# Layer 1's sixteen experts: gate and up products by seven products of quarters, the down product from turned gated rows

## What is computed

```python
def expert_choice_ffn(h, w_router, w_gate, w_up, w_down):
    b, n, _ = h.shape
    cap = CAPACITY_FACTOR * n // N_EXPERTS
    aff = jax.nn.softmax(jnp.einsum('bnd,de->bne', h, w_router).astype(jnp.float32), axis=-1)
    gate, idx = lax.top_k(jnp.swapaxes(aff, 1, 2), cap)
    bidx = jnp.arange(b)[:, None, None]
    xg = h[bidx, idx]
    hid = jax.nn.silu(jnp.einsum('becd,edf->becf', xg, w_gate)) * jnp.einsum('becd,edf->becf', xg, w_up)
    out = jnp.einsum('becf,efd->becd', hid, w_down) * gate[..., None].astype(h.dtype)
    return jnp.zeros_like(h).at[bidx, idx].add(out)
```

## Time and profile before

| | us |
|---|---|
| median of three runs | 3442.67 (3441.97 to 3445.3) |
| the profiled execution, its own time | 3441.68 |
| its span, first to last instruction | 3440.0 |
| TensorE busy (matmul) | 3204.8, 93% |
| VectorE busy | 1227.8, 36% |
| ScalarE busy | 934.1, 27% |
| GpSimd busy | 494.6, 14% |

### The profile page before, as it was taken

How to read it: one execution, slowest core, us unless ns; L and a number is a source line. 1 busy time by engine, 2 the same in 40 slices (tenths; PEclk the granted TensorE clock), 3 DMA queues, 4 the chain that set the end, 5 groups by cost and what they waited for, 6 DMA issues and landing times. The chain is left out here.

```text
span 3440.0 us, 52305 instructions
## 1 busy us (share of the span) xinstructions
PE 3204.8 (93%) x19880; PEld 2402.9 (70%) x19880; DVE 1227.8 (36%) x2978; ACT 934.1 (27%) x2163; POOL 494.6 (14%) x639
## 2 busy tenths in 40 slices
PE   6999999899977999999999799898999399999998
PEld 4888756667435878788787565665664388888886
DVE  3212178678653010110101343656784501111013
ACT  4111156755430110111101242234544111111111
POOL 0010244200100101111011210345001000000002
PEclk9999999999987999999999899999999699999999
DMA  6336353053649978777787710101314788888987
GB/s 229 129 108 118 102 198 93 15 131 99 241 148 337 338 252 273 242 266 252 260 270 240 263 60 1 61 22 39 95 33 171 257 312 314 314 315 314 316 317 275
DMA packets 389539, 672.37 MB, mean 195 GB/s; under 512 B 84040, under 2 KB 133064, under 8 KB 383168
## 3 DMA queue, kind: packets, MB, share of 16 engines
q1 hardware_dynamic: 357536, 568.00, 47.9%
q0 software_dynamic: 13616, 47.32, 5.7%
q10 hardware_dynamic: 18240, 55.16, 4.3%
HBM read 585.65 MB, written 90.97 MB: 197 GB/s over the span
## 5 line engine op out<-in xcount | busy, mean ns | idle before, releaser
L2738 PE MATMUL experts_gu_ps<-experts_xT,experts_wg 128*128 128x160 f32 (+1 forms) x4096 | 552.8, 288 | 5.1 <-DVE experts_xT L2612 2.6
L2738 PE MATMUL experts_gu_ps<-experts_xT,experts_wu 128*128 128x160 f32 (+1 forms) x4096 | 549.6, 287 | 0.0
L2738 PEld LDWEIGHTS experts_gu_ps<-experts_xT,experts_wg 128*128 128x128 f32 x4096 | 529.7, 192 | 20.1 <-issue 19.4
L2738 PEld LDWEIGHTS experts_gu_ps<-experts_xT,experts_wu 128*128 128x128 f32 x4096 | 525.2, 191 | 0.0
L2635 DVE TENSOR_TENSOR experts_hid<-experts_sil,experts_gu_ps 128x160 f32<-128x160 f32 (+1 forms) x256 | 77.9, 304 | 921.6 <-ACT experts_sil L2566 921.6
L2566 ACT ACTIVATE experts_sil<-experts_gu_ps 128x160 f32<-128x160 f32 (+1 forms) x256 | 74.3, 290 | 1100.1 <-PE experts_gu_ps L2738 1096.0
L2704 PE MATMUL experts_y_ps<-down_ahead_wd,experts_hid 128*128 128x512 f32 x512 | 228.3, 599 | 0.0
L2704 PE MATMUL experts_y_ps<-experts_wd,experts_hid 128*128 128x512 f32 x512 | 224.0, 595 | 1.2 <-DVE experts_hid L2635 1.2
L2653 DVE TENSOR_SCALAR experts_y<-experts_y_ps,experts_wt 128x512 f32<-128x512 f32 x31 | 23.3, 751 | 436.9 <-PE experts_y_ps L2704 436.9
L2704 PEld LDWEIGHTS experts_y_ps<-experts_wd,experts_hid 128*128 128x128 f32 x512 | 96.0, 190 | 118.1 <-issue 114.8
L2704 PEld LDWEIGHTS experts_y_ps<-down_ahead_wd,experts_hid 128*128 128x128 f32 x512 | 94.6, 190 | 114.4 <-issue 113.7
(11 more groups left out here) (488 smaller groups left out, 4819.6 us busy)
## 6 DMA issues: line engine op xcount, KB each, us to landing
experts_wg<-in_l_w_gate SPq DMA_DIRECT2D x64, 2048.0 KB, 8.6
experts_wu<-in_l_w_up SPq DMA_DIRECT2D x64, 2048.0 KB, 13.5
down_ahead_wd<-in_l_w_down SPq DMA_DIRECT2D x32, 2048.0 KB, 10.6
experts_wd<-in_l_w_down SPq DMA_DIRECT2D x32, 2048.0 KB, 10.9
down_ahead_wd<-in_l_w_mod SPq DMA_DIRECT2D x16, 1024.0 KB, 8.9
proj<-proj_ob ACTq DMA_DIRECT2D x60, 256.0 KB, 2.3
first_w<-in_l_w_in SPq DMA_DIRECT2D x6, 2048.0 KB, 10.1
attn_a_mod_w<-in_l_w_mod ACTq DMA_DIRECT2D x12, 1024.0 KB, 6.3
```

The costliest lines, as they stand in the source:

```text
L2738: mm = nc.tensor.matmul(GU[f % 2][:, part, 0:N], w[:, h, k, c * P:(c + 1) * P], xT[:, k, :], start=(k == 0), stop=(k == KD - 1))
```

## The change

Layer 1 gets a function of its own, `last_experts`; `experts` is now for layer 0 only, with the branches for the end never taken. `FinishAhead` no longer has a tile for the residual rows; they are loaded during the last expert into the memory of the gate weights.

For gate and for up the product of 128 rows with a 1024x1024 matrix is made by seven products of quarters (64 rows, 512 inner, 512 columns), in the order 5, 1, 2, 6, 3, 7, 4. The stationary operand is a 128x64 block of turned rows or of their sums (`sx`), the moving one 256 columns of weights or of weight sums; the two halves j of the 512 columns go to partitions 0 to 63 and 64 to 127 of one PSUM bank. VectorE makes the four sums of each weight matrix (128x2048 elements each; one of them in place) and the four sums of the rows. ScalarE copies four part results of each matrix out of PSUM (`kept`), VectorE adds the other four to them (`quarter`), and multiplies silu and up (`hidden`). The gated rows now come out unturned: TensorE turns them (`turn_hidden`, 8 transposes), ScalarE copies them to `hT`, and the down product stays 16 matmuls of 512 columns, now over k in the outer loop.

```diff
 class FinishAhead(Ahead):
-        self.x = self.sb("x", [P, NTX, D])
...
+    def load_rows(self, sp, x):
+
         for t in range(NTX):
-            sp.dma_start(self.x[:, t, :], self.res[t * P:(t + 1) * P, :]).then_inc(self.x_in, 16)
+            sp.dma_start(x[:, t, :], self.res[t * P:(t + 1) * P, :]).then_inc(self.x_in, 16)
...
+PRODUCTS = (5, 1, 2, 6, 3, 7, 4)
+KEPT = (5, 1, 6, 7)
+QUARTERS = ((0, 0, 2, 1), (0, 1, 3, 6), (1, 1, 7, 5), (1, 0, 4, 7))
...
+            def _(sp):
...
+                for i in range(3):
+                    for half in range(2):
+                        load(i, half, 0)
+                following.load(sp)
+                with sp.Fori(0, E - 1) as e:
+                    for i in (GATE, UP):
+                        sp.wait_ge(mm_done, multiplied(e, i, 7))
+                        load(i, 0, e + 1)
+                        sp.wait_ge(mm_done, multiplied(e, i, 4))
+                        load(i, 1, e + 1)
+                    for half in range(2):
+                        sp.wait_ge(y_done, START + e * 2 + (half + 1))
+                        load(DOWN, half, e + 1)
+                sp.wait_ge(mm_done, multiplied(E - 1, GATE, 4))
+                following.load_rows(sp, x)
+                sp.wait_ge(s_done, (E - 1) * 16)
...
+                for t in range(M_SLOTS):
+                    load_sum(t)
...
+            def _(act):
...
+                def gates_and_up(e, squares=()):
+                    nc.scalar.activation(unused[:], K.eps[:, 0:1], ACT.Silu)
+                    for p in KEPT:
+                        keep(e, GATE, p)
+                    act.wait_ge(dve_out, quarter_at(e, GATE, 3))
+                    nc.scalar.activation(gate[:], gate[:], ACT.Silu).then_inc(sil_done, 1)
+                    for p in KEPT:
+                        keep(e, UP, p)
+                        if p in (1, 6):
+                            for t in squares[p // 6 * 2:p // 6 * 2 + 2]:
+                                square(t)
+                    for c in range(2):
+                        act.wait_ge(ht_done, START + e * 2 + (c + 1))
+                        for h in range(2):
...
+                            nc.scalar.activation(to, here, ACT.Copy).then_inc(hid_out, 1)
...
+            def _(dve):
...
+                def weight_sum(e, i, p):
+
+                    b11, b12, b21, b22 = (quarter_of(i, low, right) for low in range(2) for right in range(2))
+                    if p == 5:
+                        for half in range(2):
+                            dve.wait_ge(w_in[i][half], START + e * 16 + 16)
+                        add = nc.vector.tensor_tensor(sums_of(i, 5), b12, b11, ALU.subtract)
...
+                def gates_and_up(e, between=None):
+                    weight_sum(e, GATE, 4)
+                    weight_sum(e, UP, 5)
+                    quarter(e, GATE, 0)
+                    quarter(e, GATE, 1)
+                    weight_sum(e, UP, 6)
+                    quarter(e, GATE, 2)
+                    quarter(e, GATE, 3)
+                    weight_sum(e, UP, 7)
+                    weight_sum(e, UP, 4)
+                    dve.wait_ge(ht_done, START + e * 2)
+                    for q in range(4):
+                        if between and q in (0, 2):
+                            between(q)
+                            between(q + 1)
+                        quarter(e, UP, q)
+                        hidden(e, q)
...
+                with dve.Fori(0, E - 1) as e:
+                    gates_and_up(e)
+                    for p in (5, 6, 7):
+                        weight_sum(e + 1, GATE, p)
+                    row_sums(e + 1)
+                    dve.wait_ge(ixs_in, START + e + 1)
+                    dve.wait_ge(y_done, START + e * 2 + 2)
+                    nc.vector.tensor_scalar(y[:, BANK:D], Y[1][:], wt[:], None, ALU.mult).then_inc(yv, 1)
...
+                gates_and_up(E - 1, gated)
+                dve.wait_ge(following.x_in, START + 16 * NTX)
+                for t in range(NTX):
+                    if t >= M_SLOTS:
+                        gated(t)
+                    summed(t)
...
+            def _(pe):
...
+                    bank = {5: Z, 3: Z, 2: W, 4: V}.get(p, X)
+                    for k in range(HALF):
+                        for j in range(2):
+                            mm = nc.tensor.matmul(bank[j * HD:(j + 1) * HD, 0:COLS], by[k], at[:, k, j, :], start=(k == 0 and p in (1, 2, 4, 5)),
+                                                  stop=(k == HALF - 1 and p in (2, 3, 4, 7)), skip_group_check=True)
+                    mm.then_inc(mm_done, 1)
...
+                with pe.Fori(0, E - 1) as e:
+                    for i in (GATE, UP):
+                        for p in PRODUCTS:
+                            multiply(e, i, p)
+                    turn_hidden(e, 0)
+                    turn_rows(e + 1)
+                    turn_hidden(e, 1)
+                    pe.wait_ge(dve_out, quarter_at(e, UP, 3))
+                    for k in range(KD):
+                        if k % HALF == 0:
+                            pe.wait_ge(hid_out, START + e * 4 + (3 + k // HALF))
+                        for h in range(2):
+                            mm = down_rows(e, k, h)
+                        if k % HALF == HALF - 1:
+                            mm.then_inc(y_done, 1)
```

286 lines of the change are left out of this document (282 added, 4 removed).

## The result

The changed kernel takes 3426.86 us (median of five runs, 3419.79 to 3427.8); the kernel before, run beside it, 3444.73 us (3441.97 to 3446.52). The ratio is 0.9946, with a 95% interval of 0.9934 to 0.9958. The change is faster by about 18 us, half a percent, where 24.7 were forecast (3442.7 to 3418). The direction was right, and the time lies in the forecast's own range of 3410 to 3428.

A forecast was written before the change was run, and what follows sets the result against it. TensorE's own work was taken to set the pace, DMA engines close behind. Start +3.8, loop -39.8, end +11.6 make -24.4 on 3440.0, a span of 3415.6; with 1.7 and 1.0 added, 3418 us, range 3410 to 3428.

The forecast's parts named there:

- rival 7: TensorE's products: weight loads stand open, 0.136 us ahead of each pair, 15 us an expert; +244, 3662 us; chance 0.01.
- rivals 6: TensorE's products: the two halves don't run side by side, a product takes 3.46 us; +387, 3805 us; chance 0.01.
- 4 (3434): TensorE's products: each product's waits cost 0.07 us somewhere, 16 us in all; 3434 us; chance 0.05.
- The new wait: TensorE before each down product: idle 0.67 us until ScalarE has copied the last turned block.
- Rival 5: VectorE in the expert loop: it is the bound, sums at 4.6 us each, 45 us an expert; 3483 us; chance 0.02.
- Rival 2: DMA engines in the expert loop: they bind, gaps lose 1.5 us more per expert, period 42.2; 3440 us; chance 0.09.
- GpSimd's queue: Scatter, then gather, per expert: issued by 19.6, rows there at 22.9, wanted at 24.8; no cost, bounds 0 to 4 us.
- rival 1: GpSimd in the expert loop: scatter and gather wait behind VectorE's sums, TensorE idles nearly 3 us; +45, 3463; chance 0.12.
- The start: Before the first expert's first product: 3.8 us later (1.8 to 6), from late gather 2.0, ScalarE's blocks 1.4, row sum 0.4.
- The end: Last expert: late residual and tiles stall product 7 of up and delay VectorE; 11.6 us more, bounds +3 and +15.
- Rival 3: Last expert: the end is milder, tiles arrive 8 us sooner; 3409 us; chance 0.10.
- The sum: Whole span: +3.8 at the start, -39.8 in the loop, +11.6 at the end, -24.4 together; span 3415.6 us.

The follow-up runs named there:

- halves apart: Changed kernel with each product's matmuls reordered, all four inner blocks of one column half before the other half's; 3461.56 us.
- the doubled sums: Changed kernel with eight extra, repeated weight sums per expert on VectorE, results unchanged; 3535.28 us.
- the short down product: Changed kernel without inner blocks 4, 5 and 6 of the down product (last expert whole), 3354.89 us; with smaller down-weight loads too, 3351.09 us.
- the version with the late gather: Changed kernel with the next expert's row gather held until product 6 of up is done; 3438.28 us.
- the version with the start wait: Changed kernel with VectorE's first two weight sums waiting until the first gather has landed; 3424.43 us.

## Why the prediction came out as it did

**What bounds the kernel** was read rightly. TensorE's own work set the pace before and does after, and the whole gain of the loop is in the length of its work: 15 x (43.35 - 40.71) = 39.6 us, the trace has 38.8 with a first step that is 2.5 us longer than the others (its first product runs at a granted clock of 0.50, as the first block did before, and takes 3.68 us as that took 3.75; the second is 0.8 us longer too) and a last one that is 0.7 longer.

**TensorE's work**: 8 x 0.216 = 1.73 us for a product, measured 1.73. The rows on which this rested came from other stages, with four groups of 32 columns and two of 64; that they carry over is what halves apart also shows. Weight loads do not stand open: rival 7 (3662) fell, and rivals 6 (3805) and 4 (3434) with it, since products start 1.73 us apart. What the Trainium skill says (TensorE: Matmul & The Clock Gate, Part 3, The mechanism), that a load overlaps only with matmuls on other rows of the array, does not hold here: both halves use all rows, and pairs are 0.216 us apart. The same section also lets a load into the background weight buffer go ahead of running matmuls; that would fit, but no run here shows which buffer a load used.

**The new wait** was put at 0.67 us; 0.52 is measured, 2.3 us over the loop in the forecast's favour. The down product and the transposes take what they took.

**VectorE**: a sum 2.3 us, measured 2.28 to 2.29; 26 us an expert, measured 25.0. It is not the bound, and the doubled sums say from where it would be. Rival 5 (3483) fell. **ScalarE** was put at about 12 us and takes 40.88 x 40.71 / 160 = 10.4.

**The DMA engines**: they work at 410 GB/s on the weights instead of 387, which the forecast did not have (below). Rival 2 (3440) fell: it wanted 1.5 us more in each expert, and 13 of the 15 steps are 40.71 us. By the short down product full DMA engines begin to cost at some 36 us.

**GpSimd's queue**: right in the sum, wrong in both parts, and not safe in every step. The forecast allowed for an issue by 19.6 and a landing of 3.3 us; in most steps the trace has an issue that begins at 13.05 to 13.3 and a landing 9.9 after that. Both give 22.9: the agreement is an accident. VectorE's sums hold the gather's issue until the running sum ends (2.7 us in the median, 1.0 before); the scatter's takes 1.60 us as before (1.63 in the earlier trace rows), but it begins ahead of the sum, so whether one would hold it these traces don't say.

What rival 1 (3463) described does happen, but seldom. In the last step, which starts at 3304.96, the scatter lands at 12.2 us instead of 11.1. With that the two small copies behind it miss VectorE's rest and are held, each by one weight sum (GpSimd's timeline):

```profile
3317.93 2.06 POOL L2897 COPY experts_wt<-experts_weight 128x1 f32 x1
3319.92 2.26 POOL L2886 COPY experts_ixg<-experts_index 128x1 int32 x1
3323.05 1.00 POOL L2889 DMA_INDIRECT experts_xg<-normed,experts_ixg  x1 [0.87 <-POOL experts_ixg L2886]
```

Otherwise they take 0.18 us each. The issue begins at 18.1, the rows are there at 25.4, TensorE waits 0.5 us, and the step takes 41.40. In the seven traces whose period is 40.71, one or two of the 14 steps after the first are like this (0.15 to 0.8 us each): always where the scatter landed at 11.9 or later. So the price of the mechanism was 0.7 us in the whole loop and not 45; the cover is 1.9 us only while the scatter is in time, and that has less than 1 us to spare. A late gather costs what it is late, as the version with the late gather shows.

The gather's issue takes 2.87 us beside a sum and 1.12 beside an idle VectorE. With that the Trainium skill agrees in kind (SBUF — State Buffer, Who interferes with whom): a VectorE instruction with two SBUF inputs keeps a GpSimd instruction that reads SBUF waiting. The section takes it that such an instruction does not stall the descriptors of a DMA, which it calls inferred; here the issue is held at its beginning, and its last 0.99 us do run beside the next sum.

**The start**: 3.8 forecast, 3.6 measured. The largest term, 2.0 for the gather, is 1.8 by the version with the start wait (12.4 - 10.6).

**The end** is the step that was mis-sized: +11.6 forecast, +15.1 measured, a hair above the bounds of +3 to +15. The next largest miss is the loop's, 1.0 us. The mechanism was the one described: the residual is asked for 12 us into the last expert, the tiles of `moe` land behind it, a copy waits behind their squares and TensorE behind the copy. Where the 3.5 us lie is seen by following VectorE, which ends last (timeline of VectorE, ScalarE and SP's queue of the changed kernel; the expert starts at 3346.36):

```profile
3385.18 4.86 DVE L3053 SCALAR_TENSOR_TENSOR experts_wg<-experts_m,experts_ms,experts_wg 128x1024 f32<-128x1024 f32 x4
...
3390.72 1.06 ACT L2943 ACTIVATE experts_sq<-experts_m 128x1024 f32<-128x1024 f32 x1 [4.05 <-DMA experts_m<-moe]
...
3393.91 1.28 DVE L3053 SCALAR_TENSOR_TENSOR experts_wg<-experts_m,experts_ms,experts_wg 128x1024 f32<-128x1024 f32 x1 [0.78 <-POOL experts_ms L2914]
...
3398.05 1.22 DVE L3048 TENSOR_TENSOR experts_m<-experts_m,finish_ahead_gate 128x1024 f32<-128x1024 f32 x1
3398.26 1.42 POOL L2914 TENSOR_TENSOR experts_ms<-experts_ms,neg_half 128x1 f32<-128x1 f32 x1
...
3399.78 1.28 DVE L3053 SCALAR_TENSOR_TENSOR experts_wg<-experts_m,experts_ms,experts_wg 128x1024 f32<-128x1024 f32 x1 [0.51 <-POOL experts_ms L2914]
3402.71 1.28 DVE L3053 SCALAR_TENSOR_TENSOR experts_wg<-experts_m,experts_ms,experts_wg 128x1024 f32<-128x1024 f32 x1 [0.51 <-POOL experts_ms L2914]
```

The quarters of up are done, and the adding of tiles begins, at 38.8 after the start instead of 37.5: the first tile was squared at 29.5, not 28, and product 7 took 3.68 us instead of 1.73, since the granted clock was 0.50 after the stall:

```profile
3378.70:3382.20 3.50, 3.47 (x17) 2.21 (x19) 3.43 (x6) 2.07 (x4) 3.27 (x7) 0.50 0.01 2
```

Tile 4 is then added by 3393.91 + 1.28, which is 48.8 instead of 46.5: 1.3 of these 2.3 us are the ones just named. Most of the rest is its load: it is asked for at 3386.48 and squared 4.2 us later, while by the forecast it was there 3.4 us after slot 0 came free. The last three tiles are 2.93 us apart (3402.71 - 3399.78) instead of 2.45, 1.4 us more: GpSimd's root is held by VectorE's product of the same tile (1.42 us instead of 0.55), ends 0.4 us after it, and VectorE waits 0.5 us for the root each time. The forecast had this row in its hands and used it for the gather, not for the tiles. These are 3.7 us, and the chain behind the tiles is 0.2 shorter than forecast. Rival 3 (a milder end, 3409) fell.

**The sum** was -24.4, the spans differ by -21.9, of which -1.8 lie ahead of the stage; in the stage it is -20.1, and -21.0 when the change was run again. So the sum was 3.4 to 4.3 us too good, and the end alone is 3.5. That the time of 3426.9 lies 8.9 above the 3418 has a second, larger reason: the change's median is 7.1 us above its profiled execution, which was its fastest, where the forecast added 1.0. In the kernel before it was 1.0 over three runs, but 3.05 over the five. That step, from one execution's own time to the median, was taken as a constant. It makes some 6 of the 8.9 us, more than any term of the sum missed by, and it was in part luck that the time still lies 1.1 us inside the range.
